# The first norm and the first two weight units of a long fused block: rounding after the root, remainders in eighths

## The reference, cut to what matters

```
def rms_norm(x, w):
    xf = x.astype(jnp.float32)
    return xf * lax.rsqrt(jnp.mean(xf * xf, axis=-1, keepdims=True) + EPS) * w.astype(jnp.float32)

h = rms_norm(x, norm_w[layer])
proj = h @ w_in + b_in          # layer 0: 35 column blocks of 128
...                             # mLSTM, sparse attention, HGRN2, two FFNs, stick breaking attention, RWKV-7
```

## Time and profile before

| | |
|---|---|
| median of 3 runs | 1012.05 us (1011.27 to 1013.35) |
| profiled execution | 1013.05 us |
| its span, first to last instruction | 1011.2 us |
| PE busy | 966.5 us (96%), 9040 matmuls |
| POOL busy | 652.3 us (65%) |
| ACT busy | 536.6 us (53%) |
| DVE busy | 462.9 us (46%) |
| DMA | 139.79 MB, mean 138 GB/s |

### The profile page before, as it was taken

One profiled execution on the slowest core, in us unless ns is written; L12 is line 12 of the kernel. 1 busy time (PEld: TensorE's weight loads), 2 busy tenths in 40 slices (PEclk: granted clock), 3 DMA queues, 4 the chain that ended last, 5 costly groups with the idle time before them and its releaser, 6 DMA issues.

```text
span 1011.2 us, 23135 instructions
## 1 busy us (share of the span) xinstructions
PE 966.5 (96%) x9040; PEld 926.9 (92%) x9040; DVE 462.9 (46%) x844; ACT 536.6 (53%) x789; POOL 652.3 (65%) x276
## 2 busy tenths in 40 slices
PE   4999999999889999999999999999999999999997
PEld 4988788889889989999999989999998989999996
DVE  5256424766565574433330133563484753334112
ACT  6577654666644676544443346765421664454441
POOL 1885333368699817977777746554313479878782
PEclk9999999999999999999999999999999999999999
DMA  8654213245433305555555544333002246555551
GB/s 333 208 156 145 85 64 104 70 161 166 147 105 104 127 22 188 175 179 172 180 170 171 178 129 146 126 107 102 3 4 86 81 160 209 183 182 187 185 180 51
DMA packets 39041, 139.79 MB, mean 138 GB/s; under 512 B 4272, under 2 KB 5552, under 8 KB 38832
## 3 DMA queue, kind: packets, MB, share of 16 engines
q1 hardware_dynamic: 38960, 138.62, 41.6%
HBM read 137.55 MB, written 1.05 MB: 137 GB/s over the span
## 4 chain that ended last, share of the span: by engine, by line
PE 56%; issue 22%; POOL 15%; DVE 4%; ACT 2%; DMA 0%; POOLq 0%; SPq 0%; DVEq 0%; ACTq 0%
PE ps L698 56%; POOL wlo L632 14%; DVE qkl L1939 1%; DVE hT L1975 1%; ACT whi L1514 1%; POOL rN L673 0%; DMA xT<-in_x 0%; ACT qkl L1440 0%; POOL dif L656 0%; ACT dif L1440 0%; ACT rstd L1440 0%; DVE aL L1985 0%; DVE mixT L1939 0%; ACT ps L1440 0%; PE ps L1247 0%
## 5 line engine op out<-in xcount | busy, mean ns | idle before, releaser
L632 POOL TENSOR_TENSOR wlo<-ring,whi 128x1024 fp32r<-128x1024 f32 x251 | 606.9, 2437 | 314.5 <-ACT whi L1514 296.3
L1514 ACT ACTIVATE whi<-ring 128x1024 fp32r<-128x1024 f32 x253 | 266.8, 1060 | 183.9 <-PE ps L698 150.0
L698 PE MATMUL ps<-aH,whi 128*128 128x272 f32 (+1 forms) x1048 | 307.8, 294 | 10.4 <-DVE aL L1985 5.5
L698 PE MATMUL ps<-aH,wlo 128*128 128x272 f32 (+1 forms) x1048 | 301.9, 288 | 0.0
L698 PE MATMUL ps<-aL,whi 128*128 128x272 f32 (+1 forms) x1048 | 301.4, 288 | 0.0
L698 PEld LDWEIGHTS ps<-aH,whi 128*128 128x128 f32 x1048 | 200.9, 192 | 16.2 <-issue 8.8
L698 PEld LDWEIGHTS ps<-aL,whi 128*128 128x128 f32 x1048 | 200.8, 192 | 0.6 <-issue 0.5
L698 PEld LDWEIGHTS ps<-aH,wlo 128*128 128x128 f32 x1048 | 200.7, 191 | 0.0
L698 PE MATMUL ps<-fxH,whi 128*128 128x256 f32 x480 | 135.5, 282 | 4.0 <-POOL wlo L632 2.4
L698 PE MATMUL ps<-fxL,whi 128*128 128x256 f32 x480 | 135.1, 281 | 0.0
L698 PE MATMUL ps<-fxH,wlo 128*128 128x256 f32 x480 | 135.0, 281 | 0.0
(11 more groups left out here) (364 smaller groups left out, 1429.8 us busy)
## 6 DMA issues: line engine op xcount, KB each, us to landing
ring<-in_stream SPq DMA_DIRECT2D x253, 512.0 KB, 3.8
cst<-in_cst SPq DMA_DIRECT2D x1, 1325.0 KB, 12.7
xT<-in_x SPq DMA_DIRECT2D x4, 272.0 KB, 3.9
out<-hT SPq DMA_DIRECT2D x4, 256.0 KB, 2.4
row<-in_row SPq DMA_DIRECT2D x1, 898.0 KB, 9.4
cst<-in_cst SPq DMA_DIRECT2D x1, 640.0 KB, 10.2
mat<-in_mat SPq DMA_DIRECT2D x1, 576.0 KB, 13.7
vec<-in_vec SPq DMA_DIRECT2D x1, 135.0 KB, 4.0
```

The source lines that it names most:

```text
L632: nc.gpsimd.tensor_tensor(wlo[:, s, :], ring[:, s, :], whi[:, s, :].bitcast(F32), ALU.subtract).then_inc(S("w_split"), 1)
L698: return nc.tensor.matmul(out, lhsT, rhs, start=start, stop=stop, skip_group_check=True)
L1514: nc.scalar.activation(whi[:, v % SLOTS, :], ring[:, v % SLOTS, :], ACT.Copy).then_inc(S("w_high"), 1)
```

## The change

The sum now takes all eight squares on DVE (seven additions) and one matmul, whose ones are a tile that POOL fills at the start (`th`, a buffer of a later stage) instead of the loaded constants. ACT rounds unit 0 right behind the root, and unit 1 behind the first `aH`. DVE subtracts units 0 and 1 in slices of 128 columns, one k at a time, inside of its loop: behind `hT[j]` come slice j of unit 0 and slice j - 1 of unit 1. Each slice goes through `step`. `feature_pair` waits at each k for the slice (`first_low`) and no longer for whole units. `w_split` is raised for unit 0 with its last slice, and for unit 1 with its last slice.

```diff
-SUMMED = {"norm0": 7, "norm1": 5, "ffn1": 7, "mix": 5, "ffn2": 7, "final": 5}
+SUMMED = {"norm0": 8, "norm1": 5, "ffn1": 7, "mix": 5, "ffn2": 7, "final": 5}
...
+            nc.gpsimd.memset(th[:, 0, 0:P], 1.0).then_inc(S("ones_set"), 1)
             pool.wait_ge(S("w_split"), 2)
             lows(2, U_H + 20)
...
             def feature_pair(u, g, t0, ready, tag=None):
                 xh, xl = acts(tag)
-                parts = [weights(u + j) + [bank(g + j)] for j in range(2)]
+                if u == U_E:
+                    parts = [[w[:, j, :].rearrange("p (k n) -> p k n", n=P) for w in (whi, wlo)] + [g % MM_BANKS + j] for j in range(2)]
+                else:
+                    parts = [weights(u + j) + [bank(g + j)] for j in range(2)]
                 for k in range(KT):
+                    if u == U_E:
+                        pe.wait_ge(S("first_low"), k + 1)
                     pe.wait_ge(S(ready[0]), ready[1] + k + 1)
...
+                ones = C("ones")
                 if i == 0:
-                    pe.wait_ge(S("early_in"), 32)
+                    ones = th[:, 0, 0:P]
+                    pe.wait_ge(S("ones_set"), 1)
                 elif tag not in LATE:
                     filler(1)
                 pe.wait_ge(S("norm_sum"), sums_up_to(tag))
-                m = mm(ps[:, 7, 0:n], C("ones"), sq[:, 0, 0:n], True, SUMMED[tag] == KT)
+                m = mm(ps[:, 7, 0:n], ones, sq[:, 0, 0:n], True, SUMMED[tag] == KT)
...
                 if tag == "norm0":
-                    high(1)
+                    high(0)
                 if tag in ("norm0", "norm1", "mix"):
                     for k in range(KT):
+                        if tag == "norm0" and k == 1:
+                            high(1)
                         act.wait_ge(S("norm_x"), ...)
                         func(aH[:, k, TT - n:TT], hT[:, k, TT - n:TT], ACT.Copy, "norm_hi")
...
                     square("norm0", k, TM, T)
-                high(0)
                 act.wait_ge(S("setup"), 6)
...
+            def first_low(u, k):
+                if k == 0:
+                    dve.wait_ge(S("w_high"), u + 1)
+                at = slice(k * P, (k + 1) * P)
+                tt(wlo[:, u, at], ring[:, u, at], whi[:, u, at].bitcast(F32), ALU.subtract, "first_low" if u else "dve_step")
+                if k == KT - 1:
+                    dve.sem_inc(S("w_split"), 1)
+                    dve_n["w_split"] = u + 1
...
                     scaled_vectors()
-                    low(0)
                 dve.wait_ge(S("norm_rstd"), NORMS.index(tag) + 1)
...
-                    if first and j == 1:
-                        low(1)
+                    if first and j == 0:
+                        first_low(0, 0)
+                    if first and j >= 1:
+                        for u, k in ((0, j), (1, j - 1)):
+                            if k < KT:
+                                first_low(u, k)
                     if first and j == KT + lag - 1:
                         forget_bounds()
```

## The result

The changed kernel takes 1022.69 us (median of 4 runs, 1021.49 to 1024.51), the kernel before 1012.34 (4 runs, 1011.27 to 1013.35): ratio 1.0095, interval 1.0081 to 1.0109. It is slower, as forecast, but by 10 us and not by 3. The profiled execution took 1021.78 us, 8.7 more than that of before.

A forecast was written before the change was run, and what follows sets the result against it. The prediction took the chain last `hT`, rounding of unit 2, POOL to bound the entry into unit 2. Slices delay it by 3.2 us, the other terms adding nothing: 1012.05 + 3.2 = 1015.3 us, range 1013.4 to 1017.7.

The forecast's parts named there:

- The root: Start of the kernel: Exp ends at 11.11 instead of 11.60, a gain of 0.5 us; `hT[0]` starts at about 11.2.
- rounding unit 0 behind the root: ACT, after Exp: 1.06 us of rounding now on the path, gain gone; PE starts at 14.59 against 14.55.
- The slices: DVE's loop: 0.32 us a slice with `step`, 1.37 us a loop step instead of 0.73; last `hT` 3.23 us later.
- the cover: Entry into unit 2: PE's first pair, done at 25.2 to 25.8, is hidden by POOL's 26.1, 0.3 us to spare at worst.
- The hand-over: Last `hT` to PE's unit 2: distances unchanged; rounding of unit 2 at 22.47, POOL at 23.68, PE at 26.13 against 22.90.
- the lower level as a rival: PE falls to its lower clock level: 1.7 us more, about 1017.0 us; chance 0.12.
- The loads: Reloads of weight slots: unit 4 issued at 22.1, landed by 26.9, rounded at 28.0, needed at 28.4; hidden by 0.4 us.

The follow-up runs named there:

- e1: The changed kernel with the four small forget_bounds operations behind the last `aL` instead of ahead of it; 1016.76 us, kernel before 1013.61.
- e8: The kernel e1 with slices of 256 columns, one for each tile instead of two of 128; 1014.92 us, kernel before 1013.78.
- e7: The changed kernel with six extra matmuls of 256 columns on PE ahead of k = 7 of the first pair; 1022.12 us, kernel before 1013.78.
- e5: The kernel before with seven extra DVE operations of 256 columns on a scratch tile behind the last `aL`, PE waiting for them; one execution, 1012.72 us.
- e3: The kernel before with four more small DVE operations ahead of the last `aL`; 1019.61 us, kernel before 1013.61.
- e6: The kernel before with POOL waiting, in the HGRN stage, for DVE's level 1 product ahead of its level 2 operations; 1014.38 us, kernel before 1013.78.
- e4: The kernel before with the sum part alone (seven additions, one sum matmul with ones made by POOL); 1014.62 us, kernel before 1013.61.

## Why the prediction was wrong

*The root.* Right: `hT[0]` at 10.86, against 11.2 foretold and 11.72 before, and PE's first product at 14.24, foretold 14.59. The 0.35 us too early are chance and not the change: in this execution the last input tiles landed 0.47 us earlier (ACT's second four squares start at 6.06, against 6.53 before), so the additions ended at 8.38, foretold 8.85. In e1 they ended at 8.75, and PE started at 14.61. As said, rounding unit 0 behind the root takes the gain back.

*The slices.* Right: 0.29 us each, and four steps of 1.38 us (1.37 foretold). That POOL starts at 23.59 (23.68 foretold) is closer than it should be: the loop began 0.34 us earlier than foretold (14.02 against 14.36), and its five steps took 7.10 us and not 6.85, for the pause in the fifth. e1 measures this term in the whole time: 1016.76 less 1013.61 is 3.2 us, as forecast. e8 shows that the price is paid for each operation.

*The step that failed* is the one on the cover, in "The hand-over": that the small operations run from 22.9 to 23.8, `aL[7]` ends at 24.2, and "POOL's 26.1 hides that too". The same paragraph has POOL starting at 23.68. I laid DVE's work and POOL's side by side, each at the duration it has alone. In the kernel before the last `aL` started 0.35 us ahead of POOL; the change puts it behind. The forecast's own figures have them overlap: four small operations from 22.9 to 23.8 and the last `aL` to 24.2, with POOL on the weights from 23.68. In place of 24.2 the last `aL` ended at 28.51. What was to cover PE's first pair, POOL's first subtraction, was what held it up.

*What it cost.* In the profile the changed kernel is 9.0 us late at unit 12, e1 3.5 (rounding of unit 12 at 48.12). The 5.5 between them are the block and what follows from it, and e7 puts 2.6 of them down to PE's lower level behind a gap of 4.87 us. 2.9 are left for the block as such (at unit 12 e7, which has the block and not the lower level, is 2.9 us behind e1). The prediction had named the lower level as a rival (1.7 us), but by the pauses within the loop and ahead of unit 2; in those of the loop PE rose to its upper level (a matmul each 0.12 us from 17.33 on) and stayed there. It fell in the long gap.

*The loads.* Unit 4 was issued at 22.03 and landed 3.7 us later, ahead of need. The cover held.

The 8.8 us of the span are not the 10.35 of the medians. The profiled execution of before lies 0.7 us above its median and that of the changed kernel 0.9 below, which makes up the difference of 1.6.

The Trainium skill has the rule that I passed over (SBUF — State Buffer, "Who interferes with whom"): DVE's second pair of SBUF ports is GpSimd's only one, and a DVE instruction with two SBUF inputs excludes a GpSimd instruction that reads SBUF, and one in a mode that uses both ports excludes GpSimd; whichever issues first holds the ports for its whole length, and the other is blocked. e5 agrees in all seven forms (2.57, 1.93 and 2.05 us against 0.42). It would have put the last `aL` behind at least one subtraction of POOL. By the trace's 2.36 us a unit that ends at 26.0 (23.68 and 2.36), with the last six matmuls still to come, and so outside of the cover.

## What to carry to other kernels

When an edit delays or moves an operation of DVE, look at what POOL runs at the new time, before calling it hidden; an operation on two SBUF tiles, or a scaling of one, can wait for whole POOL instructions, however small it is. Look in the trace for one form of DVE operation with very different durations: the long ones show the blocks that are already there. Cutting work into slices to start early pays the fixed time of each slice on the engine that then bounds, and moves what comes last in the loop.

## What I had not expected of the hardware

- Turns aren't equal. In the changed kernel, e3 and e5 a blocked operation of DVE got in at the next end of a POOL instruction each time (in the changed kernel 2.27, then 2.52 us). The one at 287.84 in the kernel before lasted 10.26 us, beside four POOL instructions (the expectation of e6 has five): three hand-overs from one POOL instruction to the next passed it by, and it ended 1.08 us after POOL stopped at 297.02, to wait for DVE. What decides that wasn't tried. POOL's row there:

```profile
292.28 4.74 POOL L632 TENSOR_TENSOR wlo<-ring,whi 128x1024 fp32r<-128x1024 f32 x2
```

- Executions of one kernel differ by 6 us and more (e4: 1011.97 to 1018.07), with PE's granted clock. Beside e5 to e8 the seven executions of the kernel before with a mean clock of 0.986 or 0.987 took 1016.84 to 1017.82 us, the 16 with 0.988 or more took 1011.80 to 1014.58. In the trace of e4 PE was granted 0.50 for 10 us in a place where the kernel before had 3.4, and e4 falls back by 3.8 us there, though its edit lies far ahead. What sets it off isn't shown. The stretch of e4:

```profile
95.70:105.70 10.00, 9.57 (x49) 7.18 (x50) 4.80 (x12) 5.61 (x15) 2.34 (x1) 0.50 0.15 54
```
